# Identity with the first transfers, activations transposed by a scaled identity, and the inverse's products on four quarters of the array

## The chip, the cores and the metric

One core of a Trainium2 chip runs the kernel. The metric is the time of one execution on the device in microseconds (us), less is better, and the median of three runs is compared. TensorE multiplies (its weight loads have rows of their own, PEld), VectorE (DVE) and ScalarE (ACT) do elementwise work and read the products from PSUM, and SyncE (SP) issues the DMA transfers, nearly all in one queue. PSUM has eight banks of 512 float32 columns on 128 partitions.

## What is computed

One decoder layer on 256 tokens of width 1024, all in float32: a mixer with two groups of eight heads (attention with forgetting, and RWKV-7), a mixture of experts with the top 4 of 32, and a gated layer embedding. Cut to what matters here:

```python
h = rmsnorm(x, mix_norm)
z = h @ w_in                                  # 1024 x 3848
# RWKV-7, per head, state S (64 x 64):
#   S_t = S_{t-1} diag(w_t) + (S_{t-1} a_t) b_t^T + v_t k_t^T ;  y_t = S_t r_t
x = x + concatenate([fox_out, rwkv_out]) @ w_out
x = x + moe_ffn(rmsnorm(x, moe_norm), ...)    # top 4 of 32 experts, 1024 -> 2 x 1024 -> 1024
x = x + sigmoid(rmsnorm(x, ple_norm) @ w_ple_gate) * (p @ w_ple_proj)
return rmsnorm(x, final_norm)
```

## The kernel before

**Start.** SyncE issues the two halves of x (`xs`), then the constants `con` (1053 KB, the 128 x 128 identity among them), the parameters `prm` (gains and the like, 34.5 KB), the first piece of `w_in`, the small weights, and the other pieces of `w_in` into a ring of six landing buffers of 2 MB. For each half b ScalarE sums the squares (L966) and forms 1/rms in two steps (L960, L961), VectorE multiplies the tokens by it into `hn` (L1242), and TensorE transposes `hn` in eight blocks of 128 x 128 against the identity (L453). The gain `mix` is applied while the transposed blocks are copied to `hT`: even k by VectorE (L1246), odd k by ScalarE (L974). The projections `z(n)` (L481, L486) follow: 8 matmuls of 256 columns for each group of 128 outputs.

**RWKV-7 in chunks of 64 tokens.** 8 heads in 4 chunks make 32 blocks of 64 x 64, two on each of 16 places: h2 = 0 on partitions 0 to 63, h2 = 1 on 64 to 127. `per_head` (L517 on, matmul at L523) multiplies all of them: 32 matmuls of 64 x 64, those of h2 = 0 from the lower row half to the lower output half, those of h2 = 1 from the upper to the upper. These are two of the four quarters of the array, on one diagonal. A triangular matrix has to be inverted: `aa` makes the first block inverse and its transpose (B8 and B14 in the program's numbers), and five levels double it. Level k has three products: q = (masked part) x B8 to PSUM banks 4 and 5, copied by ScalarE to B4 (L1059); t = B14 x B4 to banks 6 and 7; tt = B4 x B14 to banks 4 and 5. VectorE adds t to B8 and tt to B14 (L1229) and masks the part for the next level (`mq`). `matrices` makes the chunk matrices before that (`bp`, `kp`, `ma`, `mk`, `aa`), `state` runs the four chunks after it (`x`, `u`, `d`, `y`), and `heads` is the attention.

**Order.** Everything up to the experts is in an order written out by hand: `MIX_ORDER` gives the steps of all engines, and each engine's list of step numbers is derived from it. Between the products of a level stand other products as fillers: halves of projections (`zh` and `z` of one number), and the head sums `qss` and `kss` (L493). Steps in `ASIDE` other than `zh` have no TensorE work. The projections 24 and 25 wait for `qln`, ScalarE's logarithm of `qss`, since they share PSUM banks with it. ScalarE's steps `ffe` and `ffl` (L1040, L1042) belong to the forget gate and stand before `qln` (L1052) on that engine.

**Experts.** 32 experts and overflow items, 6 pieces of 2 MB each, land in nine buffers (six of the ring, three in B). The first expert's pieces are loaded during the mixer, each after the TensorE step that frees its buffer. From then on SyncE issues a piece when TensorE has counted the product that used its buffer (`s_used`). L836 are the expert products, L850 the biases, L813 the scatter of an item's rows, L707 and L712 the router's transposes and products, L734 the layer's projection.

## Time and profile before

| | |
|---|---|
| median of three runs | 1221.32 us (1221.27 to 1221.45) |
| the profiled execution | 1219.11 us |
| its span | 1217.3 us |
| TensorE busy | 1154.9 us, 95% |
| VectorE, ScalarE busy | 283.2 us, 170.7 us |
| moved by DMA | 434.87 MB, 357 GB/s over the span |
| chain that ended last | DMA 42%, TensorE 39% |

The times of runs and of the profile are of different executions; the profile tells what waits for what. A matmul of two float32 operands has two records (MATMUL) in the trace, and a transpose has one, so 32 small matmuls have 64 records. A row of the timeline merges neighbouring instructions of one line; where its engine sat idle before, the end of the row says how long and what ended it. In the page, 40 slices share the span, 30.4 us each.

### The profile page before, as it was taken

What the parts mean: (1) busy time and instruction counts of PE and PEld (TensorE: products, weight loads), DVE (VectorE), ACT (ScalarE), POOL (GpSimd) and SP (SyncE); (2) the same over time, 40 slices, a digit from 0 to 9 for tenths busy, and PEclk for the clock granted to TensorE, in tenths of its full rate; (3) what the DMA queues carried; (4) which work ended last, traced back from release to release, by engine and by line L of the source; (5) the groups of instructions that cost most, each with busy time, mean ns of one, the idle gap of its engine ahead of it and who ended that gap; (6) DMA issues with size and microseconds to landing.
All of it is one profiled execution on the core that took longest, in us unless ns stands there. A gap on an engine that the chain in (4) does not pass through costs nothing.

```text
span 1217.3 us, 16496 instructions
## 1 busy us (share of the span) xinstructions
PE 1154.9 (95%) x6852; PEld 496.8 (41%) x6852; DVE 283.2 (23%) x576; ACT 170.7 (14%) x317; POOL 0.2 (0%) x4
## 2 busy tenths in 40 slices
PE   6999998999999999999999999999999999999997
PEld 5888867443333333323333333333333333332334
DVE  2442625331211211111111111111111111111123
ACT  2321324120010000000010000000000000000114
POOL 0000000000000000000000000000000000000000
PEclk9999999989999999999999999999999999999999
DMA  9731023659999999999999999999999999999970
GB/s 381 301 139 70 3 96 106 234 233 384 430 427 428 428 429 428 429 428 429 428 429 428 428 429 430 427 427 430 430 427 427 430 429 425 430 430 427 425 317 34
DMA packets 32226, 434.87 MB, mean 357 GB/s; under 512 B 3968, under 2 KB 4096, under 8 KB 5824
## 3 DMA queue, kind: packets, MB, share of 16 engines
q1 hardware_dynamic: 32192, 434.37, 85.0%
q8 instruction: 27, 0.44, 0.1%
q14 instruction: 7, 0.06, 0.0%
HBM read 433.31 MB, written 1.05 MB: 357 GB/s over the span
## 4 chain that ended last, share of the span: by engine, by line
DMA 42%; PE 39%; ACT 0%; DVE 0%; issue 0%; SPq 0%; DVEq 0%
DMA ring<-in_we 42%; PE PS L836 27%; PE PS L921 2%; PE PS L684 2%; PE PS L798 2%; PE PS L813 2%; PE PS L850 1%; PE PS L805 1%; DMA hT<-in_wproj 1%; PE PS L734 0%; PE PS L880 0%; PE PS L860 0%; PE PS L740 0%; PE PS L493 0%; PE PS L821 0%
## 5 line engine op out<-in xcount | busy, mean ns | idle before, releaser
L836 PE MATMUL PS<-ring,FV 128*64 128x512 f32 x2304 | 515.5, 596 | 26.0 <-DMA ring<-in_we 26.0
L836 PEld LDWEIGHTS PS<-ring,FV 128*64 128x64 f32 x2304 | 158.0, 137 | 364.5 <-issue 302.1
L836 PE MATMUL PS<-B,FV 128*64 128x512 f32 x768 | 174.0, 596 | 9.4 <-DMA B<-in_we 8.7
L836 PEld LDWEIGHTS PS<-B,FV 128*64 128x64 f32 x768 | 53.0, 137 | 114.4 <-issue 98.7
L481 PE MATMUL PS<-hT,ring 128*128 128x256 f32 x416 | 93.6, 382 | 1.1 <-ACT hT L974 1.1
L481 PEld LDWEIGHTS PS<-hT,ring 128*128 128x128 f32 x416 | 78.1, 190 | 12.9 <-ACT hT L974 1.3
L1455 DVE TENSOR_SCALAR rz<-con,lora 64x64 f32<-64x64 f32 x30 | 7.4, 246 | 306.1 <-PE PS L836 306.1
L1537 DVE TENSOR_SCALAR hT<-PS 128x512 f32<-128x512 f32 x32 | 22.1, 691 | 185.6 <-PE PS L836 185.6
L1229 DVE TENSOR_TENSOR FV<-PS,prm 128x512 f32<-128x512 f32 x32 | 22.1, 691 | 184.0 <-PE PS L805 184.0
L798 PE MATMUL PS<-xq,rz 128*64 128x512 f32 x256 | 62.0, 605 | 0.0
L813 PE MATMUL PS<-B,rz 64*128 64x512 f32 x248 | 61.6, 615 | 0.0
L1134 ACT ACTIVATE FV<-PS 128x512 f32<-128x512 f32 x32 | 19.1, 597 | 298.4 <-PE PS L880 298.4
L1132 ACT ACTIVATE hT<-hT 128x512 f32<-128x512 f32 x32 | 20.2, 630 | 270.2 <-DVE hT L1529 270.2
L1138 ACT ACTIVATE B<-PS 128x512 f32<-128x512 f32 x32 | 19.1, 597 | 224.4 <-PE PS L836 224.4
L523 PE MATMUL PS<-B 64*64 64x64 f32 (+1 forms) x1088 | 37.8, 226 | 0.7 <-DVE B L1229 0.7
L523 PEld LDWEIGHTS PS<-B 64*64 64x64 f32 x1088 | 35.8, 135 | 5.9 <-issue 4.1
L813 PEld LDWEIGHTS PS<-B,rz 64*128 64x128 f32 x248 | 21.4, 186 | 39.8 <-issue 39.8
L850 PE MATMUL PS<-FG,rz 32*64 32x512 f32 x256 | 34.8, 613 | 0.9 <-DVE FV L1229 0.9
L921 PE MATMUL PS<-ring,hT 128*128 128x512 f32 (+1 forms) x80 | 28.1, 508 | 0.5 <-DVE hT L1229 0.5
L684 PE MATMUL PS<-ring,hT 128*128 128x512 f32 x64 | 28.1, 593 | 0.0
L1229 DVE TENSOR_TENSOR hT<-hT 128x512 f32<-128x512 f32 x32 | 22.1, 692 | 21.7 <-ACT hT L1132 21.6
L798 PEld LDWEIGHTS PS<-xq,rz 128*64 128x64 f32 x256 | 15.5, 136 | 24.2 <-issue 23.4
(262 smaller groups left out, 657.4 us busy)
## 6 DMA issues: line engine op xcount, KB each, us to landing
ring<-in_we SPq DMA_DIRECT2D x144, 2048.0 KB, 24.2
B<-in_we SPq DMA_DIRECT2D x48, 2048.0 KB, 29.3
ring<-in_wz SPq DMA_DIRECT2D x7, 2048.0 KB, 22.5
ring<-in_wo SPq DMA_DIRECT2D x2, 2048.0 KB, 8.1
ring<-in_wgate SPq DMA_DIRECT2D x2, 2048.0 KB, 38.7
con<-in_con SPq DMA_DIRECT2D x1, 1053.0 KB, 7.0
xq<-in_x SPq DMA_DIRECT2D x2, 512.0 KB, 4.4
ring<-in_wz SPq DMA_DIRECT2D x1, 1024.0 KB, 9.5
```

The lines of the kernel that those rows point to most:

```text
L481: mm = pe.matmul(bank(z_bank(n), SEQ), w[:, k, at:at + P], hT[:, k, :], **flags)
L523: mm = pe.matmul(f, lhs(rows, g), rhs(rows, g), start=True, stop=True)
L684: mm = pe.matmul(bank(2 * q + b), mixT[:, k, b * P:(b + 1) * P], w[:, k, :], start=(k == 0), stop=(k == KD - 1))
L798: mm = pe.matmul(PS[64 * h:64 * h + 64, 6, :], PM[:, b, :], xs[:, b, 512 * h:512 * h + 512], start=(b == 0), stop=(b == TB - 1))
L813: mm = pe.matmul(bank(2 * q + b), GTs[rows, b * P:(b + 1) * P], ysb[rows, :], start=False, stop=False, skip_group_check=True)
L836: mm = pe.matmul(PS[64 * h:64 * h + 64, bank_, :], lhs(4 * (q % 2) + k), w[:, k, h, :], start=(first and k == 0), stop=(q % 2 == 1 and k = ...
L850: pe.matmul(PS[64 * h:64 * h + 64, 6 + s, :], OHB[NE * s:NE * s + NE, :], bT[NE * s:NE * s + NE, 512 * h:512 * h + 512], start=True, stop= ...
L921: mm = pe.matmul(PS[:, 2 * q + b if c0 == 0 else 4, 0:c1 - c0], hT[:, k, b * P:(b + 1) * P], w[:, k, c0:c1], start=(k == 0), stop=(k == KD ...
L1132: act.activation(e_s, e_g, ACT.Sigmoid, scale=SALPHA).then_inc(s_sig, 1)
L1134: act.activation(aT, bank(7), ACT.Copy).then_inc(s_aT, 1)
L1229: return v.tensor_tensor(o, a, b, op)
L1537: v.tensor_scalar(e_l, bank(7), LIMIT, -LIMIT, ALU.min, ALU.max).then_inc(s_vl, 1)
```

## The change

Three parts.

1. The identity moves from `con` to `prm`. SyncE issues the first half of x, `prm`, the second half of x, the first two pieces of `w_in`, and then `con` and the small weights. `prm` gets a semaphore of its own. Instead of `hn` VectorE makes two matrices `scale_x[b]` of 128 x 128, the identity with row p times token p's 1/rms. TensorE multiplies the untouched tokens by it (16 matmuls instead of 16 transposes). The waits for `con` stand where it is first used.
2. `per_head` takes several products and issues them in turn for each place; a product that is `turned` goes to the other output half, so that it uses the other diagonal of quarters. `aa` makes the transposed matrix by 32 products of its own, to banks 6 and 7, where before VectorE masked a part of B9 that was there already. At levels 1 to 4, t (turned, banks 6 and 7) and tt (banks 4 and 5) are one step of TensorE with 64 matmuls.
3. q goes to banks 6 and 7, turned. It waits for t of the level before and the mask, no longer for tt; t and tt wait for tt of the level before. The products of `x` and `u` are turned. `sc0` waits for ScalarE's q5 instead of VectorE's t4.

SyncE's queue at the start; the names are the tensors (`wz` pieces of `w_in`, `lora`, `wff`, `wr`, `brt` small weights). Before:

```order
L318 DMA xq<-in_x 128x1024 x2
L319 DMA con<-in_con 128x2106
L320 DMA prm<-in_prm 128x69
L323 DMA ring<-in_wz 128x2048
L328 DMA lora<-in_lora 128x1024
L329 DMA wff<-in_wff 128x64
L330 DMA wr<-in_wr 128x256
L331 DMA brt<-in_brt 128x32
L323 DMA ring<-in_wz 128x4096 x5
```

And of the change, the same queue from its first transfer:

```order
L320 DMA xq<-in_x 128x1024
L321 DMA prm<-in_prm 128x197
L322 DMA xq<-in_x 128x1024
L325 DMA ring<-in_wz 128x2048
L325 DMA ring<-in_wz 128x4096
L330 DMA con<-in_con 128x1978
L331 DMA lora<-in_lora 128x1024
L332 DMA wff<-in_wff 128x64
L333 DMA wr<-in_wr 128x256
L334 DMA brt<-in_brt 128x32
L325 DMA ring<-in_wz 128x4096 x4
```

The parameters moved from fourth to second place and the constants from third to sixth, behind two weight pieces. TensorE from `aa` to q2 before (L523 are the 64 x 64 products in B, L481 and L483 projections, L493 head sums):

```order
L523 MATMUL PS<-B 64x64 [waits vector_steps_done]
L523 MATMUL PS<-B 64x64 x31
L481 MATMUL PS<-hT,ring 128x256 x4
L523 MATMUL PS<-B 64x64 [waits scalar_steps_done]
L523 MATMUL PS<-B 64x64 x31
L523 MATMUL PS<-B 64x64 [waits scalar_steps_done]
L523 MATMUL PS<-B 64x64 x31
L493 MATMUL PS<-rz,con 128x256 [waits scalar_steps_done,vector_steps_done]
L493 MATMUL PS<-rz,con 128x256 x3
L523 MATMUL PS<-B 64x64 [waits vector_steps_done]
L523 MATMUL PS<-B 64x64 x31
L481 MATMUL PS<-hT,ring 128x256 [waits scalar_steps_done]
```

The rows are q1, a half projection, t1, tt1, `qss`, q2 and the next half projection. The same stretch of the change, from q1:

```order
L530 MATMUL PS<-B 64x64 [waits vector_steps_done]
L530 MATMUL PS<-B 64x64 x31
L484 MATMUL PS<-hT,ring 128x256 x4
L530 MATMUL PS<-B 64x64 [waits vector_steps_done,scalar_steps_done]
L530 MATMUL PS<-B 64x64 x63
L496 MATMUL PS<-rz,con 128x256 [waits scalar_steps_done,vector_steps_done]
L496 MATMUL PS<-rz,con 128x256 x3
L530 MATMUL PS<-B 64x64 [waits vector_steps_done]
L530 MATMUL PS<-B 64x64 x31
L484 MATMUL PS<-hT,ring 128x256 [waits scalar_steps_done]
```

t1 and tt1 became one step of 64 matmuls that waits once, and the order around it stayed.

```diff
+    s_prm = sem("parameters_landed")
+    scale_x = [B[:, PLACE[b], 0:P] for b in range(TB)]
...
-            pe.wait_ge(s_in, 32)
+            pe.wait_ge(s_prm, 16)
             for b in range(TB):
+                pe.wait_ge(s_x[b], 16)
                 pe.wait_ge(s_dve, dve_at[f"hn{b}"])
                 for k in range(KD):
-                    mm = pe.transpose(PS[:, k, b * P:(b + 1) * P], hn[:, b, k * P:(k + 1) * P], ident)
+                    mm = pe.matmul(PS[:, k, b * P:(b + 1) * P], xs[:, b, k * P:(k + 1) * P], scale_x[b], start=True, stop=True)
...
-            def per_head(b0, lhs, rhs, n=CH):
+            def half(h2):
+                return slice(64 * h2, 64 * h2 + 64)
+
+            def per_head(*products, n=CH):
                 for g in range(16):
-                    for h2 in range(2):
-                        rows = slice(64 * h2, 64 * h2 + 64)
-                        f = PSF[rows, b0 * 512 + g * n:b0 * 512 + (g + 1) * n]
-                        mm = pe.matmul(f, lhs(rows, g), rhs(rows, g), start=True, stop=True)
+                    for b0, lhs, rhs, turned in products:
+                        for h2 in range(2):
+                            f = PSF[half(h2 ^ turned), b0 * 512 + g * n:b0 * 512 + (g + 1) * n]
+                            mm = pe.matmul(f, lhs(half(h2), g), rhs(half(h2), g), start=True, stop=True)
...
-                    fin(per_head(4, lambda rows, g: AR[rows, g, 0, :], blocks(4)), "aa0")
+                    fin(per_head((4, a0, blocks(4), 0), (6, blocks(4), a0, 1)), "aa0")
...
                 if kind == "q":
-                    pe.wait_ge(s_dve, dve_at[f"tt{k - 1}" if k > 1 else "mq1"])
-                    fin(per_head(4, blocks(1), blocks(8)), f"q{k}")
+                    pe.wait_ge(s_dve, dve_at[f"mq{k}"])
+                    if k > 1:
+                        pe.wait_ge(s_dve, dve_at[f"t{k - 1}"])
+                    fin(per_head((6, blocks(1), blocks(8), 1)), f"q{k}")
                 elif kind == "t":
                     pe.wait_ge(s_act, act_at[f"q{k}"])
-                    fin(per_head(6, blocks(14), blocks(4)), f"t{k}")
+                    pe.wait_ge(s_dve, dve_at[f"tt{k - 1}" if k > 1 else "aa"])
+                    fin(per_head((6, blocks(14), blocks(4), 1), (4, blocks(4), blocks(14), 0)), f"t{k}")
...
-                fin(v.tensor_scalar(hn[:, b, :], xs[:, b, :], col[:, 4 + b:5 + b], None, ALU.mult), f"hn{b}")
+                fin(v.tensor_scalar(scale_x[b], ident, col[:, 4 + b:5 + b], None, ALU.mult), f"hn{b}")
...
-                    link(tt(b16(14), b16(9), bc("m0T"), ALU.mult))
+                    link(tt(b16(14), banks16(6), bc("m0T"), ALU.mult))
```

## Rows read from the trace of the kernel before

**Rows 1.** The page, 40 slices: DMA busy in tenths, and GB/s.

```profile
DMA  9731023659999999999999999999999999999970
GB/s 381 301 139 70 3 96 106 234 233 384 430 427 428 428 429 428 429 428 429 428 429 428 428 429 430 427 427 430 430 427 427 430 429 425 430 430 427 425 317 34
```

**Rows 2.** Windows: length; PE, PEld, DVE, ACT, POOL busy (instructions); PEclk, DMA share, GB/s.

```profile
9.70:10.50 0.80, 0.76 (x4) 0.76 (x5) 0.00 (x0) 0.00 (x0) 0.00 (x0) 1.00 0.97 410
...
60.00:100.00 40.00, 40.00 (x348) 35.01 (x347) 16.04 (x25) 9.88 (x17) 0.00 (x0) 1.00 0.30 106
130.00:160.00 30.00, 30.00 (x658) 26.69 (x656) 16.67 (x17) 15.83 (x17) 0.00 (x0) 1.00 0.08 21
...
250.00:260.00 10.00, 8.55 (x23) 3.56 (x22) 4.41 (x22) 2.65 (x6) 0.00 (x0) 0.75 0.35 151
260.00:265.00 5.00, 4.71 (x25) 1.41 (x26) 1.09 (x5) 0.84 (x1) 0.00 (x0) 1.00 0.00 0
265.00:270.00 5.00, 5.00 (x28) 2.36 (x30) 1.05 (x4) 0.38 (x1) 0.00 (x0) 1.00 0.83 279
```

**Rows 3.** Timeline of the start: start, us, engine, line, operation, count, idle before.

```profile
0.71 0.87 SPq L318 DMA_DIRECT2D xq<-in_x  x2
...
6.12 0.20 ACT L961 ACTIVATE col<-col 128x1 f32<-128x1 f32 x1
...
6.42 0.75 DVE L1242 TENSOR_SCALAR B<-xq,col 128x1024 f32<-128x1024 f32 x1 [4.93 <-ACT col L961]
...
8.02 0.75 DVE L1242 TENSOR_SCALAR B<-xq,col 128x1024 f32<-128x1024 f32 x1 [0.84 <-ACT col L961]
...
9.74 3.41 PE L453 MATMUL PS<-con,B 128*128 128x128 f32 x16 [9.74 <-DMA prm<-in_prm]
12.06 2.04 DVE L1246 TENSOR_SCALAR hT<-PS,prm 128x256 f32<-128x256 f32 x4 [3.30 <-PE PS L453]
...
14.21 24.41 PE L481 MATMUL PS<-hT,ring 128*128 128x256 f32 x112 [1.05 <-ACT hT L974]
```

**Rows 4.** Single lines and tiles: record durations in ns (min/median/max), x's landing.

```profile
L453 PE MATMUL PS<-con,B x16: 273/421/477, 9.7 to 12.9; 128*128 128x128 f32 x16
...
DMA to landing us min/median/max: 3.9/4.4/5.0
```

**Rows 5.** Timeline of TensorE alone, both kinds of records: aa, q1, t1 with tt1, qss, q2.

```profile
115.41 2.08 PE L523 MATMUL PS<-B 64*64 64x64 f32 x64
...
123.68 2.08 PE L523 MATMUL PS<-B 64*64 64x64 f32 x64 [0.71 <-DVE B L1229]
125.69 1.99 PE L481 MATMUL PS<-hT,ring 128*128 128x256 f32 x8
127.61 3.95 PE L523 MATMUL PS<-B 64*64 64x64 f32 x128
131.49 2.00 PE L493 MATMUL PS<-rz,con 128*128 128x256 f32 x8
```

**Rows 6.** Timeline, VectorE and ScalarE: five operations after aa, t1's addition, ffl, qln.

```profile
118.75 4.87 DVE L1229 TENSOR_TENSOR B<-B,con 128x1024 f32<-128x1024 f32 x4
...
129.81 1.22 DVE L1229 TENSOR_TENSOR B<-PS,B 128x1024 f32<-128x1024 f32 x1 [0.38 <-PE PS L523]
...
132.48 0.42 ACT L1042 ACTIVATE FV<-FV 8x256 f32<-8x256 f32 x1
...
133.52 1.11 ACT L1052 ACTIVATE rz<-PS,epsc 128x1024 f32<-128x1024 f32 x1 [0.62 <-PE PS L493]
```

**Rows 7.** The chain that ended last, in order of time: start, us, what.

```profile
236.68 0.44 PE PS L707 x4
...
250.82 3.78 PE PS L734 x4
...
260.29 1.09 PE PS L850 x8
...
306.00 1.92 PE PS L813 x8
```

More of the change, by code:

```diff
@@ L114 @@
     elif kind in ("t", "tt"):
-        mixv += [f"{kind}{n}"]
+        mixv += [f"t{n}"] * (kind == "t") + [f"tt{n}"]
     elif kind == "sc":
@@ L316, in _ @@
         def _(sp):
-            for b in range(TB):
-                sp.dma_start(xs[:, b, :], t["x"][:, b * D:(b + 1) * D]).then_inc(s_x[b], 16)
-            sp.dma_start(con[:, :], t["con"]).then_inc(s_in, 16)
-            sp.dma_start(prm[:, :], t["prm"]).then_inc(s_in, 16)
+            sp.dma_start(xs[:, 0, :], t["x"][:, 0:D]).then_inc(s_x[0], 16)
+            sp.dma_start(prm[:, :], t["prm"]).then_inc(s_prm, 16)
+            sp.dma_start(xs[:, 1, :], t["x"][:, D:2 * D]).then_inc(s_x[1], 16)
             def piece(n, src, cols):
@@ L326, in _ @@
                 piece(n, t[f"wz{n}"], ZP[n][1])
[L327 removed]
+                if n == 1:
+                    sp.dma_start(con[:, :], t["con"]).then_inc(s_in, 16)
                     sp.dma_start(lora[:, :], t["lora"]).then_inc(s_aux, 16)
@@ L536, in _ @@
                     pe.wait_ge(s_act, act_at["g"])
-                    fin(per_head(4, blocks(2), eye), "vp0")
+                    fin(per_head((4, blocks(2), eye, 0)), "vp0")
                 z(n)
@@ L550, in matrices, with a0 @@
                     pe.wait_ge(s_dve, dve_at["tildes"])
-                    fin(per_head(6, blocks(4), eye), "bp0")
+                    fin(per_head((6, blocks(4), eye, 0)), "bp0")
                 elif kind == "kp":
                     pe.wait_ge(s_act, act_at["vp"])
-                    fin(per_head(4, blocks(1), eye), "kp0")
+                    fin(per_head((4, blocks(1), eye, 0)), "kp0")
                 elif kind == "ma":
                     pe.wait_ge(s_act, act_at["kp"])
-                    fin(per_head(4, blocks(4), ar, 2 * CH), "ma0")
+                    fin(per_head((4, blocks(4), ar, 0), n=2 * CH), "ma0")
                 elif kind == "mk":
                     pe.wait_ge(s_dve, dve_at["at"])
-                    fin(per_head(4, blocks(1), ar, 2 * CH), "mk0")
+                    fin(per_head((4, blocks(1), ar, 0), n=2 * CH), "mk0")
                 elif kind == "aa":
                     pe.wait_ge(s_dve, dve_at["mk"])
-                    fin(per_head(4, lambda rows, g: AR[rows, g, 0, :], blocks(4)), "aa0")
+                    def a0(rows, g):
+                        return AR[rows, g, 0, :]
+                    fin(per_head((4, a0, blocks(4), 0), (6, blocks(4), a0, 1)), "aa0")
                 elif kind == "qss":
@@ L629, in state, with both @@
             def state(kind, c):
-                def both(at, pairs):
+                def both(at, pairs, turned=0):
                     for j in range(NJ):
@@ L634, in both @@
                             for h2 in range(2):
-                                rows = slice(64 * h2, 64 * h2 + 64)
-                                mm = pe.matmul(PSF[rows, at + j * 64:at + (j + 1) * 64], lhs(rows, g, j), rhs(rows, g, j),
+                                rows = half(h2)
+                                mm = pe.matmul(PSF[half(h2 ^ turned), at + j * 64:at + (j + 1) * 64], lhs(rows, g, j), rhs(rows, g, j),
                                                start=(i == 0), stop=(i == len(pairs) - 1))
@@ L653, in state @@
                         pe.wait_ge(s_dve, dve_at[f"s{c - 1}"])
-                    mm = both(STATE_X, [(ar_(0), of(S, c % 2)), (blk_(2), blk_(3))])
+                    mm = both(STATE_X, [(ar_(0), of(S, c % 2)), (blk_(2), blk_(3))], turned=1)
                 elif kind == "u":
                     pe.wait_ge(s_act, act_at[f"x{c}"])
-                    mm = both(STATE_U, [(blk_(14), of(XU, 0))])
+                    mm = both(STATE_U, [(blk_(14), of(XU, 0))], turned=1)
                 elif kind == "d":
@@ L1058, in _ @@
                     pe_done(f"q{n}")
-                    fin(act.activation(flat(4), two(4), ACT.Copy), f"q{n}")
+                    fin(act.activation(flat(4), two(6), ACT.Copy), f"q{n}")
                 elif kind == "sc":
@@ L1262, in _ @@
             act_done("swaa")
+            v.wait_ge(s_in, 16)
             for j in range(NJ):
@@ L1349, in _ @@
                     mask_level(n + 1)
-                elif kind == "t":
-                    pe_done(f"t{n}")
-                    fin(tt(flat(8), two(6), flat(8), ALU.add), f"t{n}")
-                elif kind == "tt":
-                    pe_done(f"tt{n}")
+                elif kind in ("t", "tt"):
+                    pe_done(f"{kind}{n}")
+                    if kind == "t":
+                        fin(tt(flat(8), two(6), flat(8), ALU.add), f"t{n}")
                     fin(tt(flat(14), two(4), flat(14), ALU.add), f"tt{n}")
@@ L1629, in constants @@
     s, t = (p % CH), np.arange(CH)[None, :]
-    put("ident", p == f)
     put("blk", p // HD == f // HD)
```

22 lines of the change are left out of this document (11 added, 11 removed), and 6 rows, old and new, of the table MIX_ORDER.

## The prediction

> **What bounds the kernel now.** I read four views in this order: the slices of the page, the windows, the chain of waits, and the timeline of the first 15 us and of 115 to 136 us. The slices [rows 1] split the span in two. Up to about 270 us the DMA engines are mostly idle, and from the tenth slice to the thirty-eighth the rate stands at about 428 GB/s without a gap. So the expert part is a stream of weights that runs at the rate of the transfers; whatever TensorE does there, its end is its start plus the bytes over that rate. What sets the start is a landing buffer coming free: from 260 to 265 us nothing moves at all, and from 265 the queue is busy [rows 2]. At 260.29 TensorE begins the bias products of the first item, and the first expert products follow [rows 7]; the first buffer is free when the first of them are done. Thus a microsecond that is taken from the path to 265 us is taken from the end, and one that is taken later is not.
>
> On that path TensorE is the bound: 40.00 of 40 us in the window from 60, 30.00 of 30 in that from 130 [rows 2]. The chain of waits has almost only TensorE between 210 and 265 us. So in the mixer each TensorE microsecond that goes away counts, as long as VectorE and ScalarE deliver in time. Two places are different: before 9.74 us TensorE waits for the parameters' transfer [rows 3], and before q1 it waits 0.71 us for VectorE [rows 5].
>
> **The start.** Today the chain is: rstd of block 0 done at 6.32 (6.12 plus 0.20), VectorE's 0.75 us hn, the parameters' landing as the last at 9.74, 16 transposes in 3.41 us, then the gains into hT: the four on VectorE run from 12.06 to 14.10 and release TensorE's first projection at 14.21 [rows 3]. After the change the parameters are the second transfer, issued at about 1.15 (two issues take 0.87 us) behind half a megabyte; the same queue brought x0 in 3.9 us and x1 in 5.0 [rows 3, 4], so I put the landing at 5.1 to 6.2, before VectorE needs it at 6.42. x1 is issued half a microsecond later and lands at about 6.6, so its sum of squares starts 0.4 us later and the second scaled identity is ready at about 8.7 instead of 8.77 for hn1; TensorE needs it after 9. The scaled identity is an eighth of the columns of a 0.75 us instruction: between 0.1 and 0.75, I take 0.25, since the fixed part is some 0.1. TensorE starts at 6.7 instead of 9.74: 3.0 us earlier.
>
> Against this stands the price of the products. A transpose is one record, a matmul of two float32 operands two. The pace is 3.41/16 = 0.213 us at the start against 0.44/4 = 0.110 late in the mixer [rows 3, 7]: the first transposes run at 1.2 GHz, the later ones at 2.4. The 16 records last 421 ns in the median and the shortest 273 [rows 4], so TensorE had the higher level by the last of them, some 3 us after it began. (The granted clock of the window from 9.7 is given as 1.00 [rows 2]; the pace says otherwise, and I go by it.) The 16 new products cost 16 x 0.43 = 6.8 us at the low level or 16 x 0.215 = 3.4 us at the high one. If the clock rises 3 us after TensorE's start as it did here, 7 products run slowly (3.0 us) and 9 fast (1.9): the second block's first product is done at about 10.3, VectorE's four copies of 0.51 follow, and the projection begins at 12.45. The gain is 14.2 - 12.45 = **1.7 us**. If the clock stays low until about 12.7, the last product ends near 13.8 and the gain is nil. The bounds are 0 and 1.9; I take 1.7, the row's own delay. The first weight piece is now issued ahead of the constants, so it lands earlier than before; the constants have until the scan and `ssk`, tens of microseconds. That move costs nothing.
>
> **The levels.** q1 to tt1 in the row: a product set of 32 small matmuls takes 2.01 us (123.68 to 125.69), two in a row 3.88 (127.61 to 131.49) [rows 5]; the second costs 1.87, and 0.14 is the entry from another tile shape. A set uses two of the four 64 by 64 quarters of the array. The change lets t and tt share a set at levels 1 to 4, four quarters at once. The trace has no set of this form. The nearest rows are the bias products L850, four matmuls (eight records) on two row groups by two column groups, and the scatter L813, four matmuls on two row groups alone: 1.09 us against 1.92 [rows 7]. The scatter has four rounds of two records, 0.48 us each; at that price L850 has 2.3 rounds for its eight records, so four tiles do run at once. The bounds of the shared set are 2.01 (full overlap) and 3.88 (none). I take 2.06, near the lower one, since L850 is such a case; the gain is 3.88 - 2.06 = 1.82 per level, **7.3 us** for four.
>
> The aa step gets 32 more products of the same kind in the two idle quarters: 0 to 1.87 us more, 0.05 by the same choice. It is on the path: after aa VectorE has five operations of 1.22 us until mq1 [rows 6], the fillers cover them but for 0.71 us, so what aa takes longer q1 begins later. VectorE's own five operations stay five, one with another source.
>
> **What becomes late next.** Per level VectorE has mq, t and tt, 3 x 1.23 = 3.7 us, and TensorE after the change q 2.0, two fillers of 1.92 and 2.06 = 7.9 us. q needs t of the level before (TensorE's end plus 0.15 plus 1.22 = 1.4 us), and a filler of 1.92 stands between them; tt now runs during that filler and q. So this holds. ScalarE is closer. With q1's start as zero, t1 ends at 6.0, `qss` at 7.9 and q2 at 9.9, where before it was 11.8. The half projection zh24 waits for `qln`, and `qln` stands on ScalarE behind the forget gate's chain, which ends at 132.90 - 123.68 = 9.2 whatever TensorE does [rows 6]. With 1.11 us for `qln` that is 10.4: a wait of **0.5 us**, which did not exist before. At level 3 VectorE's `qn` and `ksqf` (three operations of at most 1.22 us each, counted at 3.3) follow tt2 and end about 1.9 us before `kss` wants them; levels 4 and 5 have room. q5 and tt5 stay as they are. The turned products of x and u have the same number and size in other quarters: nothing.
>
> **The sum.** 1.7 + 7.3 - 0.05 - 0.5 = 8.4 us. From 180 us to 265 every transfer on the path is issued on a step of TensorE or VectorE, the layer projection's before 250.82 included [rows 7], so the shift passes through whole, and the stream after it carries it to the end. The profiled execution took 1219.11 us (span 1217.3): 1210.7 by this. The median of the timed runs is 1221.32, 2.2 above it; I apply the same difference and get **1212.9**. One thing may add or take up to a microsecond: TensorE's clock is 0.75 of full in the window from 250, after the thin products and the wait for the projection, and four records of 512 columns take 3.78 us there, 0.95 each, where the scatter needs 0.48 a round [rows 2, 7]. Where that low stretch begins and ends may shift against the work. I count it at nil, with 1 us either way in the range.
>
> **The rivals.** (a) The clock stays low through all the new products: start 0 instead of 1.7. The end is 1214.6. For it: twice the work in each product and a start in another place of the clock's course. (b) The four quarters overlap in part, about 3.0 us a set, since each quarter's weights must be loaded once per 64 columns: 4 x 0.88 - 1.0 (aa) + 1.7, without the `qln` wait: 4.2 us, 1217.1. L850 speaks against it, though only with 512 columns for a load, where a load is hidden eightfold better. (c) The quarters take turns, because two of them share each row half: no gain in the levels, aa 1.9 us longer, start 1.7 shorter: 0.2 us slower, 1221.5, which is no change. For it: no row has two of the sets' small loads on one row half. Against it: in the window from 130 weight loads are busy 26.69 us beside TensorE's 30.00, so loads run under matmuls, and each load there has a row half whose matmul is still running [rows 2]. The Trainium skill (TensorE: Matmul & The Clock Gate, Part 3: Packing small matmuls) has as a rule that a weight load overlaps running matmuls only where the row group differs; by it two quarters on one row half would hinder each other and the outcome would be this rival, 1221.5. The trace does not bear the rule out for the pairs. (d) Slower: if changing from one diagonal to the other costs what the entry to another tile shape costs, 0.14 us, each of a set's 16 head blocks pays it twice: 16 x (0.24 + 2 x 0.14) = 8.3 us a set, 4 x 4.4 + 6.3 - 1.7 = 22 us, 1243. It decides from 3.85 us a set on. Against it: L850's four matmuls lie on both diagonals and show no such gaps. (e) The change does less than it says because ScalarE or VectorE is late in more places than `qln`: 1 to 2 us of the 8.4 lost, which lies within the range.
>
> **How the numbers follow.** Forecast 55%: 1212.9, own range 1211.3 to 1214.3 (clock stretch, copies, e). (a) 20%: 1214.6. (b) 10%: 1217. (c) 10%: 1221.5. (d) 5%: 1243. The range that leaves out 2 in 10 takes in the forecast, (a) and most of (b): 1210.9 to 1218. A measurement of this kernel can tell 0.2%, 2.4 us. Faster by more than that: forecast, (a) and nearly all of (b), 0.84. Within: (c) and the rest of (b), 0.11. Slower: 0.05.
>
> **What would show it.** In the changed kernel's timeline: the first TensorE record at 6.7 and the projection at 12.5 (14.2 under a); each t row with 128 records in about 2.1 us (3.0 under b, 3.9 under c); one wait of 0.5 us before the half projection after q2, released by ScalarE's `qln`; first expert products 8.4 us earlier and the stretch at 428 GB/s as long as before. I am wrong if the stream starts earlier and ends where it did, which would mean a bound that I do not see, or if TensorE shows new waits for VectorE between 124 and 175 us.

## The result, and the profile after

The changed kernel takes 1210.42 us (median of 4 runs, 1209.16 to 1211.20) where the kernel before took 1221.30 (4 runs, 1220.86 to 1221.45) beside it: a ratio of 0.9913 with a 95% interval of 0.9899 to 0.9926, 10.9 us. The forecast was 1212.9 with a range from 1210.9. So the direction was right and the gain was larger than the range allowed, by 0.5 us at its lower end. In a second set of five runs on another chip the same kernel took 1212.32. Over the experiments the kernel before was run 83 times: 1218.6 to 1224.2, median 1220.9. The profiled executions show 9.1 us between the spans (1217.3 and 1208.2).

The page of the changed kernel, the 40 slices of 30.2 us: granted clock, DMA busy, GB/s.

```profile
PEclk9999999999999999999999999999999999999999
DMA  9732033669999999999999999999999999999970
GB/s 382 304 139 73 3 141 147 231 260 377 431 426 429 429 427 430 428 429 429 428 428 429 427 429 429 429 429 428 429 429 427 429 429 429 429 427 429 428 308 35
```

Against [rows 1] the stream of 428 GB/s begins in the same slice of a shorter span and is as long as before. The distance from the first to the last expert product is 913.0 us before and 913.1 after. So nothing was gained or lost in the stream, and the 9.1 us lie ahead of its start, as forecast.

The timeline of the start (start, us, engine, line, operation, count, idle before):

```profile
0.71 0.40 SPq L320 DMA_DIRECT2D xq<-in_x  x1
1.17 0.42 SPq L321 DMA_DIRECT2D prm<-in_prm  x1
1.64 0.42 SPq L322 DMA_DIRECT2D xq<-in_x  x1
...
5.03 1.06 ACT L981 ACTIVATE hT<-xq 128x1024 f32<-128x1024 f32 x1 [2.22 <-DMA xq<-in_x]
...
6.83 0.29 DVE L1257 TENSOR_SCALAR B<-prm,col 128x128 f32<-128x128 f32 x1 [5.34 <-ACT col L976]
7.04 1.06 ACT L981 ACTIVATE hT<-xq 128x1024 f32<-128x1024 f32 x1 [0.31 <-DMA xq<-in_x]
...
7.27 5.56 PE L456 MATMUL PS<-B,xq 128*128 128x128 f32 x32 [7.27 <-DVE B L1257]
...
11.37 2.04 DVE L1260 TENSOR_SCALAR hT<-PS,prm 128x256 f32<-128x256 f32 x4 [2.24 <-PE PS L456]
...
13.52 2.83 PE L484 MATMUL PS<-hT,ring 128*128 128x256 f32 x12 [0.69 <-ACT hT L989]
```

TensorE began 2.47 us earlier than in [rows 3] and the first projection only 0.69 us earlier: the 32 records of the products took 5.56 us where the 16 of the transposes took 3.41.

The timeline of TensorE alone, `aa` to the q of level 3, answers to [rows 5]:

```profile
114.72 2.10 PE L530 MATMUL PS<-B 64*64 64x64 f32 x128
...
123.02 2.08 PE L530 MATMUL PS<-B 64*64 64x64 f32 x64 [0.72 <-DVE B L1244]
125.03 1.99 PE L484 MATMUL PS<-hT,ring 128*128 128x256 f32 x8
126.95 2.09 PE L530 MATMUL PS<-B 64*64 64x64 f32 x128
128.98 1.99 PE L496 MATMUL PS<-rz,con 128*128 128x256 f32 x8
130.90 2.08 PE L530 MATMUL PS<-B 64*64 64x64 f32 x64
133.38 1.97 PE L484 MATMUL PS<-hT,ring 128*128 128x256 f32 x8 [0.40 <-ACT rz L1067]
135.28 2.09 PE L530 MATMUL PS<-B 64*64 64x64 f32 x128
```

A joint set of 128 records takes 2.03 us (126.95 to 128.98), a set of 64 takes 2.01: the second pair of quarters is all but free. The wait for `qln` is there with 0.40 us, and it is the only new one in these rows. Up to q5 (164.34 before, 156.70 after) the levels gave 7.64 - 0.66 = 6.98 us.

The chain of waits at the end of the mixer, of the changed kernel and, below, of the kernel before (start, us, what):

```profile
236.83 5.20 DMA hT<-in_wproj
242.03 0.04 issue
242.07 2.85 PE PS L749 x4
...
251.13 1.09 PE PS L865 x8
252.22 3.58 PE PS L851 x16
```

```profile
244.45 6.32 DMA hT<-in_wproj
250.77 0.04 issue
...
261.37 3.58 PE PS L836 x16
```

From the issue of the layer projection's transfer to the first expert product it is 16.92 us before and 15.39 after. That is 1.53 us which the forecast counted at nil. In both traces TensorE waits for this transfer (0.80 us before, 0.45 after), so the stretch falls into two parts. The transfer took 6.32 us from issue to landing before and 5.20 after: 1.12 us. From the projection's first product (250.82 in [rows 7], and 242.07) to the first expert product it is 10.55 and 10.15 us: 0.40 us. The windows over this stretch (length; PE, PEld, DVE, ACT, POOL busy; PEclk, DMA share, GB/s), before and after:

```profile
244.00:250.00 6.00, 6.00 (x45) 5.62 (x43) 2.20 (x11) 2.19 (x6) 0.00 (x0) 0.86 0.98 412
250.00:256.00 6.00, 5.20 (x11) 2.37 (x12) 1.61 (x9) 0.19 (x1) 0.00 (x0) 0.58 0.59 252
```

```profile
237.00:243.00 6.00, 5.55 (x45) 5.00 (x43) 2.70 (x14) 2.19 (x6) 0.00 (x0) 1.00 1.00 423
243.00:249.00 6.00, 6.00 (x16) 2.20 (x15) 3.16 (x17) 1.22 (x4) 0.00 (x0) 0.72 0.46 194
```

The granted clock is half (1.2 instead of 2.4 GHz) in both, for 6.8 us before ((1 - 0.86) x 6 + (1 - 0.58) x 6 = 3.4 us of lost clock) and for 3.4 us after ((1 - 0.72) x 6 = 1.7). Before, it was low from about 248.3, ahead of the landing at 250.77, so part of what it cost lay beside the wait for the transfer. The three parts together are 0.66 (q1's start) + 6.98 + 1.53 = 9.2 us, the distance of the first expert products (261.37 and 252.22).

### The profile page after: what moved, and what is told of

It reads as the page before. It is cut to its first block, busy times and chain, and to the rows that moved or that the text cites. A ratio compares the mean times of both kernels' runs of the same rounds, so it can differ in the third digit from the quotient of the medians.

```text
span 1208.2 us, 16663 instructions
## 1 busy us (share of the span) xinstructions
PE 1148.4 (95%) x6932; PEld 490.3 (41%) x6932; DVE 282.4 (23%) x576; ACT 170.8 (14%) x317; POOL 0.2 (0%) x4
## 4 chain that ended last, share of the span: by engine, by line
DMA 42%; PE 39%; ACT 0%; DVE 0%; issue 0%; SPq 0%; DVEq 0%
DMA ring<-in_we 42%; PE PS L851 27%; PE PS L936 2%; PE PS L699 2%; PE PS L813 2%; PE PS L828 2%; PE PS L865 1%; PE PS L820 1%; PE PS L749 0%; PE PS L895 0%; DMA hT<-in_wproj 0%; PE PS L875 0%; PE PS L755 0%; PE PS L496 0%; PE PS L836 0%
## 5 line engine op out<-in xcount | busy, mean ns | idle before, releaser
L530 PE MATMUL PS<-B 64*64 64x64 f32 (+1 forms) x1152 | 30.4, 225 | 0.7 <-DVE B L1244 0.7
L530 PEld LDWEIGHTS PS<-B 64*64 64x64 f32 x1152 | 28.4, 135 | 6.0 <-issue 4.8
```

What stands on the lines that cost most here:

```text
L530: mm = pe.matmul(f, lhs(half(h2), g), rhs(half(h2), g), start=True, stop=True)
```

## Experiments

Each kernel was timed in five rounds and profiled. The times are medians, and the kernel before was run with each set (1221.4, 1220.8, 1221.0, 1220.3, 1220.9). "Mean clock" is the granted clock over the span that each run states. It does not count the start, where TensorE is slow in all kernels. It does count a low stretch at the very end, behind TensorE's last product, which costs no time and differs from profile to profile (1.3 to 2.9 us of lost clock, 0.001 to 0.002 of the mean). In the kernel before, where that product ended at 1209.5:

```profile
1213.00:1217.30 4.30, 0.00 (x0) 0.00 (x0) 0.67 (x1) 0.38 (x1) 0.00 (x0) 0.64 0.66 244
```

So the figure tells of the router only roughly. The profiled runs with 6.8 us of low clock there have 0.995 or 0.996, those with 3.4 us 0.996 to 0.998, and those with none 0.998 or 0.999.

**The start alone.** The kernel before with part 1 of the change.

```diff
-            for b in range(TB):
-                sp.dma_start(xs[:, b, :], t["x"][:, b * D:(b + 1) * D]).then_inc(s_x[b], 16)
-            sp.dma_start(con[:, :], t["con"]).then_inc(s_in, 16)
-            sp.dma_start(prm[:, :], t["prm"]).then_inc(s_in, 16)
+            sp.dma_start(xs[:, 0, :], t["x"][:, 0:D]).then_inc(s_x[0], 16)
+            sp.dma_start(prm[:, :], t["prm"]).then_inc(s_prm, 16)
+            sp.dma_start(xs[:, 1, :], t["x"][:, D:2 * D]).then_inc(s_x[1], 16)
...
-                    mm = pe.transpose(PS[:, k, b * P:(b + 1) * P], hn[:, b, k * P:(k + 1) * P], ident)
+                    mm = pe.matmul(PS[:, k, b * P:(b + 1) * P], xs[:, b, k * P:(k + 1) * P], scale_x[b], start=True, stop=True)
```

> The kernel before with the start of the change alone: identity in the parameters, constants later, 16 products by the scaled identity. In the changed kernel's profile the first projection began at 13.52 us instead of 14.21. Theory S (shifts pass through whole and the start is worth 0.7): first projection at about 13.5, first expert product 0.7 earlier, time 0.5 to 1 us below before. Rival P (the prediction's term): 1.7 us. Rival T (the timed runs gain more than the profile because the start moves everything against TensorE's clock): 2 to 3 us below before in the timed runs.

Measured 1217.15 (1215.05 to 1219.32, 12 runs), 0.9968 of before (0.9957 to 0.9979), 4.2 us. In its trace the first projection began at 13.95, 0.26 us earlier than before. So neither the 0.7 nor the prediction's 1.7 is what the time shows, and of the three the figure is nearest to rival T, though beyond its 2 to 3 us. The profile has 1.94 us to the first expert product (259.43 against 261.37): 0.26 from the start, 1.27 because the projection's transfer took 5.05 us instead of 6.32, and 0.41 behind its landing, where the low clock lasted 3.4 us. The clock at the router shows in the times too: 0.996 in five runs, whose median is 1218.96, and 0.998 or 0.999 in four, 1215.05 to 1216.19. A further part shows only when the starts of all profiles are compared. The first 5 us of projections (windows as above), in the kernel before and in the kernel before with the transfer first (below), whose starts are the same program:

```profile
14.00:19.00 5.00, 4.79 (x22) 4.28 (x23) 0.65 (x3) 0.39 (x1) 0.00 (x0) 1.00 1.03 439
```

```profile
14.00:19.00 5.00, 4.79 (x14) 3.99 (x15) 0.11 (x1) 0.00 (x0) 0.00 (x0) 1.00 1.02 433
```

The second has 14 records where the first has 22: its clock was still low (the granted clock reads 1.00 in every start, so the pace has to be read). Of the seven profiles whose start has transposes, three had the high clock with the first projection and four got it only at about 17 to 19 us. In the three of these four that have the old start, all that follows came 1.6 to 2.3 us later than in the profile of before, with extra products taken off. All nine profiles with the scaled product had the high clock by 13.5 us. The profile of before is one of the three, so the prediction could not see this part of the start's worth. Why the clock rises so late in some executions is open.

**The levels alone.** The kernel before with parts 2 and 3.

```diff
-                    fin(per_head(6, blocks(14), blocks(4)), f"t{k}")
+                    fin(per_head((6, blocks(14), blocks(4), 1), (4, blocks(4), blocks(14), 0)), f"t{k}")
```

> The kernel before with the levels of the change alone (aa with its own transpose, t and tt as one set, q and the states turned). Theory S: each joint set about 2.03 us, wait of about 0.4 us for qln, so q5 comes 6.9 to 7.0 us earlier than before and the end 7 us earlier, 1214.3. Rival T: 8 to 10 us earlier, since the layer projection's transfer (6.3 us before, 5.2 after) and the stretch of low clock (6.8 us before, 3.4 after) change with the levels rather than with the start.

Measured 1212.84 (1209.86 to 1215.15, 6 runs), 0.9938 (0.9924 to 0.9951), 8.5 us. The mixer's part is as expected: the joint set takes 2.03 us and the wait for `qln` 0.40. The rest is again the router's stretch, 15.1 us (237.34 to 252.42) in its profile instead of 16.9. Of these 1.84 us the transfer's shorter time (4.97 us) is 1.35, and the products behind its landing are 0.50.

**The two products of a joint set one after the other.** The changed kernel with two lines exchanged.

```diff
-                for g in range(16):
-                    for b0, lhs, rhs, turned in products:
+                for b0, lhs, rhs, turned in products:
+                    for g in range(16):
```

> The changed kernel with one edit: the two products of a joint set are issued one after the other (all 32 of one diagonal, then all 32 of the other) and not in turn for each place. If the gain of the levels is the overlap of four quarters, aa takes 3.9 us instead of 2.1 and each of the four joint sets 3.9 instead of 2.03: 1.9 + 4 x 1.85 - 0.4 (the qln wait is covered again) = 8.9 us later than the changed kernel, 1219.3. If the gain came from fewer waits and from tt being off the path, it stays near 1211.

Measured 1218.60 (1216.67 to 1220.98, 12 runs). That is 6.3 to 8.2 us over the changed kernel (1212.32 and 1210.42), against 8.9 expected. TensorE alone in its timeline, `aa`, q1, t1 with tt1:

```profile
115.00 3.77 PE L530 MATMUL PS<-B 64*64 64x64 f32 x128
124.95 2.08 PE L530 MATMUL PS<-B 64*64 64x64 f32 x64 [0.70 <-DVE B L1244]
128.88 3.78 PE L530 MATMUL PS<-B 64*64 64x64 f32 x128
134.51 2.08 PE L530 MATMUL PS<-B 64*64 64x64 f32 x64
```

The same 64 products with the same waits take 3.78 instead of 2.09 us when the quarters on one diagonal come first. The gain of the levels is the overlap of the two products of a joint set, and it needs them to be issued in turn. By these rows 5 x 1.69 - 0.4 = 8.0 us would follow, and q5 does begin that much later, 164.92 against 156.70 less 0.27 for the start; the rest of what is missing is within the spread of the runs. Both orders go from one row half to the other with every product. What differs is how soon the same quarter is used again, and also how soon the same PSUM bank is, since the two products of a joint set write to different banks. No run separates these two.

**The old transposes with the early identity.** The changed kernel with `hn` and one-record transposes.

```diff
-                    mm = pe.matmul(PS[:, k, b * P:(b + 1) * P], xs[:, b, k * P:(k + 1) * P], scale_x[b], start=True, stop=True)
+                    mm = pe.transpose(PS[:, k, b * P:(b + 1) * P], hn[:, b, k * P:(k + 1) * P], ident)
...
-                fin(v.tensor_scalar(scale_x[b], ident, col[:, 4 + b:5 + b], None, ALU.mult), f"hn{b}")
+                fin(v.tensor_scalar(hn[:, b, :], xs[:, b, :], col[:, 4 + b:5 + b], None, ALU.mult), f"hn{b}")
```

> The changed kernel with the early identity but the old way of turning the tokens: VectorE scales them (0.75 us a half) and TensorE transposes with one record per block. Theory: the scaled identity loses more in records than it saves on VectorE. x0 lands at 5.0, hn0 is done near 7.6 and hn1 near 9.7; the second half's first transpose is done near 10, VectorE's four copies of 0.51 follow, first projection at about 12.2 instead of 13.5: 1.3 us better than the changed kernel, 1209.1. Rival (VectorE's longer step was the bound and the records lie beside it): first projection at 13.5 to 14, no gain or a loss up to 0.5.

Measured 1213.61 (1212.09 to 1215.14, 6 runs), 0.9940 of before (0.9928 to 0.9953), where the changed kernel has 0.9931 (0.9916 to 0.9946) on another chip: 1.3 us slower by the medians, which is not clear of the spread, and certainly not the 1.3 faster that was expected. In its profile the first expert product begins at 254.91, in the changed kernel's two at 252.22 and 253.15. TensorE's rows and the windows behind them:

```profile
7.95 1.94 PE L456 MATMUL PS<-prm,B 128*128 128x128 f32 x8 [7.95 <-DVE B L1257]
11.47 1.94 PE L456 MATMUL PS<-prm,B 128*128 128x128 f32 x8 [1.57 <-DVE B L1257]
```

```profile
14.00:19.00 5.00, 4.80 (x11) 3.87 (x12) 0.10 (x1) 0.00 (x0) 0.00 (x0) 1.00 1.02 408
19.00:24.00 5.00, 5.00 (x24) 4.40 (x23) 0.91 (x2) 0.56 (x2) 0.00 (x0) 1.00 1.03 431
```

Eight transposes, a pause of 1.57 us for x's second half (it landed at 8.8), eight more, and the clock stayed low until about 19.2: 11 projection records in the first 5 us and 24 in the next. The projections lost about 2.4 us by this. The pause is not needed for it: the three late starts named above had 16 transposes without one. With the scaled product the pause was absent or short (0.35 us at most) and the clock never rose that late. So its second record may be more than a price; what it does to the clock is seen in nine profiles against seven, and not shown by the times.

**The changed kernel again**, on the chip of the next three.

> The changed kernel once more, on the chip of the other runs of this set, so that their medians have a base. Theory D (the 2.5 us beyond the forecast come from the stretch between the issue of the layer projection's transfer and the first expert product, which took 15.84 us in the profile of before and 13.9 to 14.3 in five later profiles, because TensorE's low clock lasts 6.8 us there against 3.4): time 1210 to 1212. Rival L (luck of four runs): 1212.9, which is the sum of the terms.

Measured 1212.32 (1211.94 to 1212.83), 0.9931 (0.9916 to 0.9946). Luck has a part: this is 0.6 us from the forecast, and all five runs have a mean clock of 0.996 or 0.997, where three of the first four had 0.998 or 0.999. The profile gives the sum with other terms than forecast, 0.16 for the start, 6.93 for the levels and 1.13 for the stretch at the router (0.72 of it the transfer). The 15.84 us of the expectation end at the bias products; to the first expert product it is the 16.92 above. The median over the nine runs is 1211.94.

**Filling products between the router's.** Two products of 512 columns into a free bank, in the kernel before and in the changed one.

```diff
             x_transposes(1, 1)
+            pe.matmul(bank(2), ident, xs[:, 0, 0:PW], start=True, stop=True)
             pe.wait_ge(s_act, act_at["T10"])
...
+            pe.matmul(bank(2), ident, xs[:, 0, 0:PW], start=True, stop=True)
             pe.wait_ge(s_ple, 32)
```

> The kernel before with two products of 512 columns (0.86 us each at the high clock, to a free PSUM bank, result unused) between the thin router products and the wait for the layer projection. Theory D: TensorE is busy where the clock fell, so the low stretch shortens from 6.8 us to 3.4 or nothing and the end comes 1.5 to 3 us earlier than before although there is more work: 1218.5 to 1220. Rival: the clock has no part, the two products cost between nothing and 1 us: 1221.4 to 1222.4.

> The changed kernel with the same two products in the same place. Theory D: its low stretch is 3.4 us already, so the fill gains less than in the kernel before, 0 to 1.5 us, and before and changed with fill lie 7.6 to 9 us apart instead of 10.9. Rival: fill does nothing or costs up to 1 us in both, and they stay 10 to 11 apart.

Measured 1218.36 (1216.13 to 1221.43, 11 runs) for the kernel before with fill, 0.9985 (0.9972 to 0.9997): 2.4 us less with more work. The changed one took 1210.98 (1208.63 to 1213.01, 5 runs), 1.3 less than without. All 16 runs have a mean clock of 0.998 or 0.999, and neither trace has a low stretch at the router. The fill also takes the wait for the projection's transfer away in both: TensorE reaches the projection only when the transfer has landed. With both gone the kernels lie 7.4 us apart by their medians and 8.5 by their ratios to before (0.9985 and 0.9915), so the effect of the change without the router's part is known to a microsecond or two. The two profiles have 5.9 us, the levels' 7.0 less 1.0, because in this one the changed kernel's first projection began at 14.79 against 13.81.

**The layer projection's transfer ahead of piece 4**, in the changed kernel and in the kernel before.

```diff
-            sp.wait_ge(s_pe, pe_at["xo10"])
-            first_item(4)
             sp.wait_ge(s_pe, pe_at["xo11"])
             sp.dma_start(wproj0.rearrange("p k n -> p (k n)"), t["wproj"][0]).then_inc(s_ple, 16)
+            first_item(4)
             first_item(5)
```

> The changed kernel with the layer projection's transfer (512 KB) issued ahead of the first item's piece 4 (2 MB), both after xo11, where piece 4 was issued at xo10 and stood ahead. If that transfer sets the start of the expert part, it lands about 2 us earlier (3 us after its issue instead of 5.2), TensorE's wait of some 0.7 us before the projection goes and the low stretch shrinks: 1 to 2 us earlier than the changed kernel. If the selection on VectorE ends as late, nothing. If piece 4 now comes late for item 0, slower.

> The kernel before with the layer projection's transfer ahead of piece 4. Theory D (between the router and the first expert product before loses to the late transfer and to 6.8 us of low clock what the changed kernel loses less of): stretch from the transfer's issue to the first expert product 13.1 us instead of 16.9, no low clock there, and the time 4 to 5 us below before, 1216 to 1217; then the same edit on the changed kernel (1208.3) is 7.5 to 8.5 below it, which is the change without that stretch. Rival: 2 us or less below before, and the 2 us beyond the forecast come from somewhere else.

The changed kernel with this order takes 1208.33 (1207.68 to 1209.19, 4 runs), 0.9900 (0.9881 to 0.9918) of before: 4.0 us below the changed kernel on the same chip, and the fastest of the study. The wait for the transfer is gone, and the clock did not fall. The kernel before with the same edit gained only 1.1 (1219.89, 11 runs), where 4 to 5 were expected. Its chain has no wait for the transfer either, but in its profile the clock fell for 6.8 us all the same. The windows of the former and of the latter:

```profile
237.00:243.00 6.00, 6.00 (x48) 5.40 (x47) 2.79 (x14) 2.19 (x6) 0.00 (x0) 1.00 0.84 317
243.00:249.00 6.00, 5.17 (x20) 1.89 (x18) 3.98 (x19) 2.82 (x6) 0.00 (x0) 1.00 1.02 434
```

```profile
246.00:252.00 6.00, 6.00 (x46) 6.00 (x45) 2.32 (x12) 2.19 (x6) 0.00 (x0) 0.82 0.83 319
252.00:258.00 6.00, 6.00 (x12) 2.31 (x13) 2.15 (x12) 1.01 (x3) 0.00 (x0) 0.61 1.01 431
```

TensorE is without a gap in 246 to 252 and still its clock fell, behind the router's transposes and thin products (32 columns, L711 in this kernel). The same products ran in the former without a fall. So theory D as I had put it, that the late transfer makes the clock fall, is wrong: no gap is needed. Two of the 11 runs had a mean clock of 0.998, and these took 1215.97 and 1215.45, the 5 us that had been expected of all.

**The parameters behind x, and both orders together.**

```diff
             sp.dma_start(xs[:, 0, :], t["x"][:, 0:D]).then_inc(s_x[0], 16)
-            sp.dma_start(prm[:, :], t["prm"]).then_inc(s_prm, 16)
             sp.dma_start(xs[:, 1, :], t["x"][:, D:2 * D]).then_inc(s_x[1], 16)
+            sp.dma_start(prm[:, :], t["prm"]).then_inc(s_prm, 16)
```

> The changed kernel with the parameters (100 KB) issued behind both halves of x. In five profiles with the parameters between the halves, x0 landed at 5.0 to 5.3 us (4.61 in before) and x1 at 7.0 to 9.8 (before 6.2), and the first projection began at 13.5 to 14.8. Theory X (the parameters' small packets and the weight pieces behind delay x): x0 lands at 4.6, x1 at 6 to 7, TensorE waits for the parameters until 7 to 8; first projection at 13 to 13.5, time 0.5 us below the changed kernel. Rival (the parameters land as late as in before, past 9): first projection at 15, 1 us slower than the changed kernel.

> The changed kernel with the layer projection's transfer ahead of piece 4 and the parameters behind x. By theory X and the measured 1208.3 of the projection's order alone: 1207.5 to 1208.3. If the order at the start costs, 1209.

Measured 1212.39 (1210.16 to 1214.09) and 1209.68 (1208.74 to 1213.60). x0 landed at 4.64 as before, and the parameters at about 7.2, so TensorE began at 7.64. The first projection came at 14.82 us (14.46 in the second), with the parameters between at 13.3 to 14.8, because the clock rose only at 13.5. The two orders at the start cannot be told apart by their times.

**The same work later.** The kernel before with two and with four extra projection products of 0.43 us, whose results the real ones overwrite, at about 63 us.

```diff
+                if n == 12:
+                    for _ in range(2):
+                        pe.matmul(bank(z_bank(n), SEQ), w[:, 0, at:at + P], hT[:, 0, :], start=True, stop=True)
                 for k in range(4 * halves[0], 4 * halves[-1] + 4):
```

> The kernel before with two extra products of 256 columns (0.43 us each, overwritten by the real ones) in the thirteenth projection, at about 60 us: all that follows comes 0.86 us later. If moving the router's stretch in time changes how long the clock is low there, some runs have a mean clock of 0.997 or more and the time is below before + 0.9, perhaps below before. If not, 1221.0 + 0.9 = 1221.9 and a clock of 0.995 to 0.996 in all runs.

> The same with four extra products, 1.7 us later. If the place in time matters, its clock figures and time differ from those of two extra products by other than 0.86 us; if not, 1222.7 with 0.995 to 0.996 in all runs.

With two the kernel takes 1218.01 (1216.53 to 1222.90, 9 runs), 0.9983 (0.9971 to 0.9995) of before: 2.9 us faster by doing 0.86 us more. With four it takes 1220.64 (1217.34 to 1223.61, 12 runs), 1.000 (0.9989 to 1.001). Seven of the nine runs with two have a mean clock of 0.998 or more, four of the twelve with four, and none of the 83 of the kernel before. The chain and the windows of the run with two:

```profile
246.89 5.00 DMA hT<-in_wproj
251.94 1.98 PE PS L737 x4
...
260.41 3.58 PE PS L839 x16
```

```profile
246.00:252.00 6.00, 5.75 (x47) 5.11 (x46) 2.16 (x10) 2.19 (x6) 0.00 (x0) 1.00 1.01 426
252.00:258.00 6.00, 6.00 (x21) 2.35 (x21) 3.90 (x21) 1.63 (x5) 0.00 (x0) 1.00 0.63 270
```

The stretch is 13.52 us long instead of 16.92, with the same instructions: 1.32 us less in the transfer (5.00 instead of 6.32) and 2.08 less behind its landing, where the clock is now high. This profile is not a clean shift by 0.86 us, though. Its clock at the start rose late, so the stretch began 2.44 us later than in the profile of before. What the runs show is in their number: a mean clock of 0.998 or more, which the kernel before never had, came in seven of nine with 0.86 us more work ahead. So the place in time has a part. That it alone decides is not shown: in the kernel before with the transfer first the stretch began 1.7 us later than in before, and the low clock lasted 6.8 us as there.

**One filling product with the best order.** The changed kernel, the transfer's order as above and the first of the two filling products.

> The changed kernel with the layer projection's transfer ahead of piece 4 and one filling product of 512 columns (0.86 us) ahead of the second half's router products. If the filling keeps the clock up in every run: mean clock 0.998 to 0.999 in all, 1208.3 + 0.9 = 1209.2, steadier than without it. If the clock stays up without it as in 1208.33's four runs, it only costs 0.9. If it lets the clock fall less often than without it, below 1208.3.

Measured 1209.01 (1208.44 to 1210.41, 5 runs), mean clock 0.998 to 0.999 in all. It costs 0.7 against the four runs without it, which had no low stretch either, and may be worth it where the clock does fall.

The router's stretch in all profiles, from the issue of the layer projection's transfer (or the transposes T10, which begin with it) to the first expert product:

| low clock in the stretch | length of the stretch in us, by profile |
|---|---|
| 6.8 us | before 16.9; transfer first in before 16.5, in both orders 16.5; parameters behind x 16.5 |
| 3.4 us | changed 15.4 and 15.8; start alone 15.2; levels alone 15.1; in turn 15.3; transposes 15.0; four extra products 16.3 |
| none | two extra products 13.5; transfer first 13.1; with one fill 13.9, with two 14.8 and 14.8 (0.86 us each) |

The low clock of 6.8 us costs 16.5 - 13.1 = 3.4 us with one and the same order of transfers, where the transfer is not waited for. In the kernels whose TensorE waits for the transfer its landing is in the figures as well: 6.3 us after the issue in before, 6.1 with four extra products, 5.0 to 5.6 in the changed kernel, start alone, levels alone, in turn, transposes and two extra products.

## Why the prediction was right and wrong

**The bound** was right: the end moved with the first expert product and the stream kept its length, 913.0 and 913.1 us.

**The start** was mis-sized: 1.7 us forecast, 0.69 in the profile. Small things took the rest. x0, which I had left at its old landing, landed 0.42 us later with the parameters between the halves (5.03 against 4.61; over the profiles 4.9 to 5.3 with this order and 4.6 to 4.7 with the others, with one 5.3 among them). VectorE's small scaling took 0.29 instead of 0.25, for which I had no row, and TensorE began 0.15 us behind its end, at 7.27 and not 6.7. And the clock rose 3.7 us after TensorE's start, not 3.0. In the seven profiles with the scaled identity and the parameters between the halves, the first projection began between 13.3 and 14.8 us (five of them by 13.95). In the six with the old start it began between 13.8 and 14.2. The other end of my bounds, no gain, is as near to these as the profile's 0.7. The landing of x's second half lay between 7.0 and 9.0 in them. Against this the prediction had no term for the late rise of the clock with the old start (three profiles of six, 1.6 to 2.3 us), since the profile of before does not have it. It makes the start worth more in the timed runs than the profile says.

**The levels** were right: 7.3 - 0.05 - 0.5 = 6.75 forecast, 6.98 measured. The joint set was taken at 2.06 and is 2.03, and the wait for `qln` at 0.5 and is 0.40. Rivals (b), (c) and (d), a set that overlaps in part, not at all or with a loss, are refuted by the row of 2.09 us. The Trainium skill's rule on weight loads (TensorE: Matmul & The Clock Gate, Part 3: Packing small matmuls), that they overlap running products only in other row groups, would have made the set 3.9 us as the prediction read it. The loads of a joint set, two on each row half, cost nothing beside those of a single set (2.03 against 2.01 us), so the measurement decides against that reading here. Nor does the rule separate 3.78 from 2.09, since both orders alternate between the row halves; the order in which the two products are issued does.

**The first step that failed** is the last one of the path, "so the shift passes through whole", together with "I count it at nil". The stretch from the issue of the projection's transfer to the first expert product gave 1.53 us in the profile. The larger part, 1.12 us, is the transfer itself, whose time I had taken as fixed: it landed 6.32 us after its issue before and 5.20 after. Why it took longer before is open. The low clock, which I had named, gave the other 0.40. I had its row (0.75 of full clock) and allowed it 1 us either way, though four records alone took 3.78 us there. The row itself has (1 - 0.75) x 10 = 2.5 us of lost clock, and the stretch from 244 us on has 3.4, so 1 us was too narrow a bound. Each of the 83 runs of the kernel before has a mean clock of 0.995 or 0.996, so by the profiles none was free of the low clock at the router; the changed kernel, with 0.996 to 0.999, has runs of more than one kind. No run tells what decides how long it lasts, only that 0.86 us more work ahead shortens it in most runs.

**The second step that failed, and the larger one**, is the offset: the profiled execution of before lay 2.2 us below the median of its runs, and I carried that difference over to the changed kernel, whose profiled execution lay 0.4 below. Of the 2.5 us by which the median missed the forecast these are 1.8. The terms make up the other 0.7: 1.0 too much for the start, 0.2 too little for the levels, 1.5 too little for the stretch at the router. What the offset stands for is shown in part. A profile is one execution, and executions of one kernel differ in the late rise of the clock at the start, in the transfer's landing, in the low clock at the router, and in the stream, where the first expert product to the last takes 912.5 to 915.9 us over the profiles. How much of each is in a median, no run tells. The second comparison, 8.5 us against the forecast's 8.4, hits the number with the same wrong terms, so the hit is luck.

## What to carry over

Small products that leave quarters of the array idle should be issued in turn over all four quarters: 64 products cost what 32 did (2.03 against 2.01 us), while the same products diagonal by diagonal cost 3.78. A thin stretch on the critical path, where TensorE is busy with short products or waits, should be looked up in the granted clock before any shift of the work ahead of it is priced, since the stretch can lengthen or shorten by more than the shift. One profile is one execution: a difference of 2 us between it and the median is no constant that can be added to another kernel. A small transfer that someone waits for belongs ahead of the 2 MB ones: together with a clock that stayed up it took this kernel from 1212.3 to 1208.3.

## What was not expected of the hardware

More work made the kernel faster twice: two filling products (2.4 us) and two extra products some 185 us ahead of the router (2.9 us). At the start the clock rose by 13.5 us in all nine profiles with two-record products, and in four of seven with transposes only at about 17 to 19; the one pair of kernels that differs in this alone, the transposes with the early identity against the changed kernel, is not apart clear of the spread of its times. The Trainium skill (TensorE: Matmul & The Clock Gate, Part 1: The HAM clock gate) says that the point of the change of clock varies from run to run; the starts agree with it, with a rise some 3 us after TensorE's first transposes in three profiles and 7 to 9 us in three others with the same start, and so does the changed kernel, which had all values of the mean clock from 0.996 to 0.999. The kernel before, with 0.995 or 0.996 in all of its 83 runs, varied less than that at the router.
